# A mixture-of-experts kernel whose expert weights pass through a ring of 12 places: 18 places, six experts loaded ahead in place of four, and x1 kept in DRAM

## What is computed

```python
scores = sigmoid(t @ w_router); sel = scores + router_bias     # t: 256 x 1024, 64 experts
# group-limited: 4 of 8 groups, then the top 8 experts of each token
act = silu(g) * u * combine                                    # g, u = split(t @ w_gate_up[e])
routed = sum over experts of act @ w_down[e]                   # 1024x512 and 256x1024 weights per expert
shared = (silu(sg) * su) @ w_shared_down
x = x1 + gate2 * (routed + shared); y = rmsnorm(x, final_norm_g)
```

| experts | tokens |
|---|---|
| 58, 59 | 32, 11 |
| 60 to 63 | 32, 8, 0, 52 |
| the other 58, sorted | 81 79 67 64 / 64 64 64 64 63 60 60 60 59 56 56 54 51 51 46 43 42 42 39 38 35 35 / 34 32 30 29 29 25 25 23 22 22 20 20 17 16 14 14 14 13 13 11 11 10 7 5 5 4 3 3 3 1 1 0 |

## Time and profile before

### The profile page before, as it was taken

The page is one execution under the profiler, slowest core; times in us unless marked ns, Lnnn a source line. Parts: engine busy times, 40 slices in busy tenths (PEclk is TensorE's granted clock), DMA queues, the critical chain, the costliest instruction groups (busy, mean ns, idle before and its releaser), DMA issues.

```text
span 936.0 us, 12460 instructions
## 1 busy us (share of the span) xinstructions
PE 840.4 (90%) x5100; PEld 566.1 (60%) x5100; DVE 361.5 (39%) x719; ACT 199.5 (21%) x314; POOL 107.8 (12%) x69
## 2 busy tenths in 40 slices
PE   4699999998999999999999989699787998779974
PEld 2488998678999988888455434255242553435422
DVE  1327899279798441156212122012121121112214
ACT  3124443033434120033112111011110111101101
POOL 1000628222342210021000000000000000000000
PEclk9799999999899999979999999899898999989987
DMA  8978887222252439731869999999999999999991
GB/s 319 387 266 317 317 287 256 90 90 90 91 180 92 152 117 346 279 134 46 313 266 417 419 416 418 415 418 419 415 418 416 416 420 414 419 415 415 419 401 59
DMA packets 76419, 280.46 MB, mean 300 GB/s; under 512 B 5080, under 2 KB 7496, under 8 KB 59976
## 3 DMA queue, kind: packets, MB, share of 16 engines
q1 hardware_dynamic: 76008, 278.90, 76.2%
q10 hardware_dynamic: 352, 0.74, 0.2%
HBM read 277.52 MB, written 2.10 MB: 299 GB/s over the span
## 4 chain that ended last, share of the span: by engine, by line
PE 76%; DMA 15%; DVE 4%; SPq 2%; issue 2%; ACT 1%; POOL 0%; DVEq 0%; POOLq 0%
PE bank L1766 14%; DMA chunk<-in_w_expert_down 11%; PE bank L1813 11%; PE bank L1417 9%; PE bank L1665 5%; PE bank L1429 5%; PE bank L1431 5%; PE bank L1437 5%; PE bank L1688 4%; PE bank L1472 3%; PE bank L1452 3%; DMA ring<-in_w_ada 2%; PE bank L1385 2%; DMA chunk<-in_w_expert_gate_up 2%; PE bank L1653 2%
## 5 line engine op out<-in xcount | busy, mean ns | idle before, releaser
L1766 PE MATMUL bank<-chunk,xg 128*32 128x512 f32 (+2 forms) x1024 | 193.6, 627 | 25.9 <-DMA chunk<-in_w_expert_gate_up 25.5
L1766 PEld LDWEIGHTS bank<-chunk,xg 128*32 128x32 f32 (+2 forms) x1024 | 63.8, 131 | 152.7 <-issue 138.4
L1813 PE MATMUL bank<-chunk,act_t 128*32 128x512 f32 (+2 forms) x512 | 108.3, 710 | 26.2 <-DMA chunk<-in_w_expert_down 22.2
L1270 DVE SCALAR_TENSOR_TENSOR act_r<-bank,w_slot,sil 128x256 f32<-128x256 f32 x26 | 12.6, 484 | 190.1 <-ACT sil L837 190.1
L1813 PEld LDWEIGHTS bank<-chunk,act_t 128*32 128x32 f32 (+2 forms) x512 | 33.0, 143 | 81.4 <-issue 81.3
L571 POOL TENSOR_TENSOR small<-small 128x4 f32<-128x4 f32 (+2 forms) x9 | 10.2, 1136 | 607.4 <-DVE small L1326 502.8
L1282 DVE TENSOR_TENSOR y_lo<-bank,y_hi 128x512 fp32r<-128x512 f32 x52 | 36.0, 692 | 107.5 <-ACT y_hi L850 107.5
L850 ACT ACTIVATE y_hi<-bank 128x512 fp32r<-128x512 f32 x52 | 31.1, 597 | 125.0 <-PE bank L1813 125.0
L837 ACT ACTIVATE sil<-bank 128x256 f32<-128x256 f32 x26 | 10.0, 385 | 205.7 <-PE bank L1766 205.7
L1665 PE MATMUL bank<-sel_p,h_hi 128*128 128x256 f32 x208 | 52.7, 294 | 0.9 <-DVE act_s L1226 0.9
L961 DVE SCALAR_TENSOR_TENSOR conv<-upad,dw,conv 128x256 f32<-128x256 f32 x120 | 51.2, 501 | 0.0
(11 more groups left out here) (269 smaller groups left out, 1318.9 us busy)
## 6 DMA issues: line engine op xcount, KB each, us to landing
chunk<-in_w_expert_gate_up SPq DMA_DIRECT2D x128, 1024.0 KB, 17.2
chunk<-in_w_expert_down SPq DMA_DIRECT2D x64, 1024.0 KB, 18.6
ring<-in_w_in SPq DMA_DIRECT2D x16, 2048.0 KB, 10.5
ring<-in_w_ada SPq DMA_DIRECT2D x12, 2048.0 KB, 14.2
ring<-in_w_proj_hgrn SPq DMA_DIRECT2D x2, 2048.0 KB, 8.0
ring<-in_w_out SPq DMA_DIRECT2D x2, 2048.0 KB, 12.8
ring<-in_w_proj_conv SPq DMA_DIRECT2D x1, 2048.0 KB, 7.7
w_sg<-in_w_shared_gate_up SPq DMA_DIRECT2D x1, 2048.0 KB, 9.7
```

Source lines behind the costliest of these rows:

```text
L1766: ins = mm(bank[2 + b][e * width:(e + 1) * width, :], xg[:, k, c:c + width], w[:, k % 4, :], start=(k == 0), stop=(k == KD - 1))
L1813: ins = mm(out[e * width:(e + 1) * width, :], act_t[:, c, e * width:(e + 1) * width], w[:, c, h * 512:(h + 1) * 512], start=(c == 0), stop ...
```

## The change

The ring gets 18 places, at addresses given one by one in `PLACES`. Six experts are fixed, in three steps; 58 are ranked, with 4, 22 and 32 of them in the three widths. `STEPS` keeps its 26 steps and sums (four of width 128, fourteen of 64, eight of 32) in another order. The shared expert's down weights become piece 48, just ahead of those of step 6, and its product moves from step 1 to step 6. `x1` is written to a DRAM tensor and read back after the last piece, as `fin_g` is; `g2row` is formed in steps 24 and 25.

```diff
-FIXED, WIDE, MIDDLE, NARROW = 4, 4, 24, 32
+FIXED, WIDE, MIDDLE, NARROW = 6, 4, 22, 32
-STEPS = [64, 64] + [32, 128, 64, 64, 32, 64] * 4
+FIXED_STEPS = FIXED // 2
+STEPS = [64] * FIXED_STEPS + [32, 64, 32, 128, 64, 32, 64, 64, 32, 128, 64, 32, 64, 64, 32, 128, 64, 32, 64, 128, 32, 64, 64]
...
-NCHUNK = 12
+NCHUNK = 18
+SHARED_STEP = 6
 CHUNK_NO = {}
 for n_step, n_items in enumerate(ITEMS_OF):
+    if n_step == SHARED_STEP:
+        CHUNK_NO["shared"] = len(CHUNK_NO)
     for n_part in range(3):
         for n_item in range(n_items):
             CHUNK_NO[n_step, n_part, n_item] = len(CHUNK_NO)
 CHUNK_AT = {number: key for key, number in CHUNK_NO.items()}
...
+PLACES = [152, 112, 120, 80, 88, 0, 8, 144, 16, 24, 72, 32, 40, 48, 56, 160, 168, 64]
+AFTER_SHARED = (15, 16)
+EXTRA_PLACES = 12
+LOADS_BEFORE_EXTRAS = (len(CHUNK_NO) - EXTRA_PLACES) // NCHUNK + 1
...
-        chunk = [at(f"chunk{i}", 8 * i, [P, 2048]) for i in range(NCHUNK)]
-        h_hi = at("h_hi", 112, [P, NS, KD, P], F32R)
-        h_lo = at("h_lo", 120, [P, NS, KD, P], F32R)
-        x1 = at("x1", 128, [P, NS, D])
-        xg = at("xg", 144, [P, KD, 2 * P])
+        chunk = [at(f"chunk{i}", PLACES[i], [P, 2048]) for i in range(NCHUNK)]
+        x1_out = at("x1_out", 128, [P, NS, D])
+        h_lo = at("h_lo", 128, [P, NS, KD, P], F32R)
+        h_hi = at("h_hi", 136, [P, NS, KD, P], F32R)
+        xg = at("xg", 96, [P, KD, 2 * P])
...
-        w_sg = at("w_sg", 144, [P, KD, 2 * FF])
-        w_sd = at("w_sd", 104, [P, 2, D])
+        w_sg = at("w_sg", 160, [P, KD, 2 * FF])
...
-        fin = at("fin", 96, [P, NS, D])
-        fin_sq = at("fin_sq", 112, [P, NS, D])
+        fin = at("fin", 48, [P, NS, D])
+        fin_sq = at("fin_sq", 56, [P, NS, D])
+        g2row = at("g2row", 64, [P, NS, D])
+        fin_g = at("fin_g", 160, [P, D])
+        x1 = at("x1", 168, [P, NS, D])
...
-            first = 3 * NE // NCHUNK - NIT
-            eng.wait_ge(s_chunk[extra_place(b, part, item)], i * 16 + 16 * (first + 1))
+            eng.wait_ge(s_chunk[extra_place(b, part, item)], i * 16 + 16 * (LOADS_BEFORE_EXTRAS + 1 - NIT))
...
-                               ("t1", 4, "act"), ("g2", 4, "act"), ("hr", 4, "act"), ("sg", 1, "act"), ("su", 1, "dve")]):
+                               ("t1", 4, "act"), ("hr", 4, "act"), ("sg", 1, "act"), ("su", 1, "dve")]):
...
-                if name == "ph1":
-                    evacuated(sp, "st", 3)
-                    sp.dma_start(new_state[0, 0].rearrange("a h k v -> k (a h) v"), s_new[:, :, :]).then_inc(s_state, 16)
...
+            evacuated(sp, "st", 3)
+            sp.dma_start(new_state[0, 0].rearrange("a h k v -> k (a h) v"), s_new[:, :, :]).then_inc(s_state, 16)
+            sp.dma_start(w_sg[:, :, :], cols(A["w_shared_gate_up"][0], 0)).then_inc(s_sg, 16)
...
             for number in range(NCHUNK):
-                step, part, item = CHUNK_AT[number]
-                if number == 0:
+                if number in AFTER_SHARED:
+                    continue
+                if number == 1:
+                    sp.wait_ge(o_ready, 4)
+                if number == 4:
                     sp.wait_ge(ob_used, 4)
-                if number == 2:
+                if number == 5:
                     released(sp, "ph0")
-                if number == 4:
+                if number == 7:
                     released(sp, "ph1")
-                    sp.dma_start(w_sg[:, :, :], cols(A["w_shared_gate_up"][0], 0)).then_inc(s_sg, 16)
-                    sp.dma_start(fin_g[:, :], A["final_norm_g"].rearrange("(a d) -> a d", a=1).broadcast_to([P, D])).then_inc(s_fing, 16)
-                if number == 6:
+                if number == 10:
                     sp.wait_ge(merged, 4)
-                if number == 7:
+                if number == 11:
                     released(sp, "wo0")
-                if number == 9:
+                if number == 13:
                     released(sp, "wo1")
-                load_part(number, part, FIRST_FIXED + sum(ITEMS_OF[:step]) + item)
+                load_fixed(number)
+            evacuated(sp, "t1", 3)
+            sp.dma_start(A["x1"].rearrange("s p d -> p s d"), x1_out[:, :, :]).then_inc(s_x1_kept, 16)
             filled(sp, "su")
-            sp.dma_start(w_sd[:, :, :], A["w_shared_down"][0].rearrange("(k p) c -> p k c", p=P)).then_inc(s_sd, 16)
+            for number in AFTER_SHARED:
+                load_fixed(number)
 
...
+                if CHUNK_AT[number] == "shared":
+                    sp.wait_ge(shared_done, 1)
+                    return
...
-            for step in range(2, NSTEPS):
+            for step in range(FIXED_STEPS, NSTEPS):
+                if step == SHARED_STEP:
+                    number = CHUNK_NO["shared"]
+                    freed(number - NCHUNK)
+                    sp.dma_start(dn_tile(place_of(number)), A["w_shared_down"][0].rearrange("(c p) d -> p c d", p=P)).then_inc(s_chunk[place_of(number)], 16)
...
+            for number in (max(n for n in CHUNK_AT if place_of(n) == at_) for at_ in (15, 16)):
+                freed(number)
+            sp.dma_start(fin_g[:, :], A["final_norm_g"].rearrange("(a d) -> a d", a=1).broadcast_to([P, D])).then_inc(s_fing, 16)
+            sp.wait_ge(s_x1_kept, 16)
+            sp.dma_start(x1[:, :, :], A["x1"].rearrange("s p d -> p s d")).then_inc(s_x1_back, 16)
...
+                if j == 0:
+                    pool.wait_ge(s_x1_kept, 16)
...
-            for name, dst in (("t1", x1), ("g2", g2row)):
-                if name == "g2":
-                    act.wait_ge(spread2, 1)
-                    nc.scalar.activation(inv2[:, :], bank[5][:, 0:T], ACT.Copy).then_inc(inv2_done, 1)
-                for s in range(NS):
-                    for hf in range(2):
-                        filled(act, name, 2 * s + hf)
-                        nc.scalar.activation(dst[:, s, hf * 512:(hf + 1) * 512], fill_bank(name, 2 * s + hf)[:, :], ACT.Copy).then_inc(act_evac, 1)
+            for s in range(NS):
+                for hf in range(2):
+                    filled(act, "t1", 2 * s + hf)
+                    nc.scalar.activation(x1_out[:, s, hf * 512:(hf + 1) * 512], fill_bank("t1", 2 * s + hf)[:, :], ACT.Copy).then_inc(act_evac, 1)
+            act.wait_ge(spread2, 1)
+            nc.scalar.activation(inv2[:, :], bank[5][:, 0:T], ACT.Copy).then_inc(inv2_done, 1)
...
+            def second_gate(j):
+
+                act.wait_ge(g2_ready, j + 1)
+                nc.scalar.activation(g2row[:, j // 2, j % 2 * 512:(j % 2 + 1) * 512], bank[0 if j == 3 else 1][:, :], ACT.Copy).then_inc(g2_evac, 1)
...
             for n in range(NSTEPS):
+                if n == NSTEPS - 2:
+                    second_gate(0)
+                    second_gate(1)
+                if n == NSTEPS - 1:
+                    second_gate(2)
+                    second_gate(3)
...
+            dve.wait_ge(s_x1_back, 16)
+            dve.wait_ge(g2_evac, 4)
...
-            for j in range(4):
-                s, hf = j // 2, j % 2
-                b = open_fill("g2", j)
-                for i in range(4):
-                    ins = mm(b[:, i * P:(i + 1) * P], mod_v[:, M_GT2 + 4 * hf + i, s:s + 1].broadcast_to([P, P]), ident, start=True, stop=True)
-                ins.then_inc(proj_ready, 1)
...
-            def scatter(b, s, h, last=False):
+            def scatter(b, s, h, first=False, last=False):
                 for part in (y_hi, y_lo):
-                    ins = mm(y_acc[s][h][:, :], sel_t[b][:, s * P:(s + 1) * P], part[h][:, :], start=False, stop=(last and part is y_lo))
+                    ins = mm(y_acc[s][h][:, :], sel_t[b][:, s * P:(s + 1) * P], part[h][:, :], start=(first and part is y_hi), stop=(last and part is y_lo))
...
-                pe.wait_ge(items_done, 2)
-                pe.wait_ge(s_sd, 16)
+                number = CHUNK_NO["shared"]
+                pe.wait_ge(s_chunk[place_of(number)], 16 * (number // NCHUNK) + 16)
+                w_sd = dn_tile(place_of(number))
                 for s in range(NS):
                     for hf in range(2):
                         for c in range(2):
-                            mm(y_acc[s][hf][:, :], act_s[:, c, s * P:(s + 1) * P], w_sd[:, c, hf * 512:(hf + 1) * 512], start=(c == 0), stop=False)
+                            ins = mm(y_acc[s][hf][:, :], act_s[:, c, s * P:(s + 1) * P], w_sd[:, c, hf * 512:(hf + 1) * 512], start=False, stop=False)
+                ins.then_inc(shared_done, 1)
+
+            def second_gate(j):
+
+                s, hf = j // 2, j % 2
+                if j == 3:
+                    pe.wait_ge(pt_evac, NSTEPS)
+                elif j:
+                    pe.wait_ge(g2_evac, j)
+                for i in range(4):
+                    ins = mm(bank[0 if j == 3 else 1][:, i * P:(i + 1) * P], mod_v[:, M_GT2 + 4 * hf + i, s:s + 1].broadcast_to([P, P]), ident, start=True, stop=True)
+                ins.then_inc(g2_ready, 1)
 
             def gather_next(i, weights):
...
```

(46 more changed lines are left out.)

39 lines of the change are left out of this document (19 added, 20 removed).

## The result

The changed kernel takes **957.05 us** (median of 4 runs, 955.62 to 958.5) against 937.45 for the kernel before in 4 runs: ratio 1.0204, interval 1.0183 to 1.0226. It is slower by 19.6 us; 957.0 was forecast. The runs of the changed kernel spread over 2.9 us. The profiled execution is the fastest of them: 955.62 us, span 953.5.

A forecast was written before the change was run, and what follows sets the result against it. Expert-weight DMA, not TensorE, was taken to bound half the span. Step 25's down at 903.1 plus 37.6 for the round gives 940.7; 15.0 behind it gives span 955.7, or 957.0 us on the median, range 949 to 970.

The forecast's parts named there:

- idle DMA at 475 to 485: Queue hole early in the experts' stream: moving the shared product makes it 7.1 us less, leaving some 2 us.
- step 25's down ends: End of the 26 regular steps on TensorE: at 903.1, 17.9 us earlier than 920.97.
- entry into the round: After step 25: its results, reading nwork and branching, a gather and turn; 6.2 us, bounds 5 and 8.
- the round's two steps: Extra-item steps on TensorE: 14.1 us for the first and 13.5 without a gather, 27.6 us.
- eight rounds passed over: Unused rounds of the extra-item loop, counted ahead of the last down: 3.8 us, bounds 0 and 9.4.
- the whole round: One round of extra items for two overflowing tokens after step 25: 37.6 us, range 32.6 to 45.
- behind the last down: Results, norm and stores from the last down to the span's end: 15.0 us, as before.
- 5 us of cover for the round's pieces: The round's 12 pieces, 30.2 us of DMA, land at 930.3 before the last down at about 935, so they hide.
- punctual pieces: Low-bound term: pieces land without the 3.4 us lateness allowed at the stream's end, -2.6 us.
- rival 2: Each round passed over stalls TensorE's instruction stream: 970 us, 987 if both jumps stall; middle 975, chance 0.06.
- Rival 1: No extra round runs, as rank 26's expert has at most 32 tokens or the branch is not taken: 919.3, chance 0.07.
- Rival 3: The deeper ring is not full by 448 because SP waits earlier; 12.6 us gain lost: 970 us, chance 0.04.

The follow-up runs named there:

- experiment 7: The kernel before with the second gate's four groups moved to steps 24 and 25: 935.56 us, ratio 0.9997.
- experiment 1: The changed kernel without the round of extra items, leaving out two of one expert's 34 tokens: 916.91 us, ratio 0.9805.
- experiment 2: The kernel before with 1 added to nwork, so one round runs on items that hold no token: 971.85 us, ratio 1.0406.
- experiment 10: The changed kernel timed again, unaltered, against the kernel before: 955.47 us, ratio 1.0213.
- experiment 3: The changed kernel with NX = 4 in place of 36, so the loop has one round and none is passed over: 949.84 us, ratio 1.0163.
- experiment 4: The changed kernel with 4 added to nwork, so two rounds run, the second without tokens: 985.99 us, ratio 1.054.
- experiment 6: The kernel before with the shared expert's down product moved from step 1 to step 6: 930.37 us, ratio 0.9935.
- experiment 5: The changed kernel without the round, two tokens left out, with 12 pieces loaded early in place of 18, ring still 18: 923.03 us, ratio 0.9863.

## Why the prediction was right

| step of the prediction | predicted | measured |
|---|---|---|
| start of the stream | 447.9, as before | 446.25 |
| idle DMA at 475 to 485 | 2 us (7.1 less) | 0.9 us |
| step 25's down ends | 903.1 | 901.16 |
| last byte of the round's pieces | 926.9 | 926.3 |
| the second gate in steps 24 and 25 | 1 + 2 groups of 0.93 us in the sum | 1.09 and 1.98 us in the chain, but no cost in experiment 7 |
| entry into the round | 6.2 us (5 to 8) | 5.2 us |
| the round's two steps | 27.6 us | 27.9 us |
| eight rounds passed over | 3.8 us (0 to 9.4) | 3.98 us; in place of 0.48, so 3.5 us more |
| the whole round | 37.6 us | 37 to 38 us by experiments 1, 2 and 10 |
| without it | 919.3 (17.9 us under before) | 17.9 us under before by the medians, 18.3 (15.4 to 21.2) by the ratio |
| last down ends | 940.7 | 934.30 |
| behind the last down | 15.0 us | 19.2 us |
| span | 955.7 | 953.5 in the profiled run, the fastest of four |

The mechanism was the one forecast. The decisive step was not in the trace's timing but in its counts: 1024 records said that nothing overflowed before, and the sorted counts said that one expert, with 34 tokens in a width of 32, overflows now. Experiment 1 shows that this alone turns a gain of 17.9 us into a loss of 19.6. The sums agree to a microsecond partly by luck: the start of the stream and step 25 came out 1.7 and 1.9 us early, and the profiled span is 2.2 us below the predicted one, while the median run is 1.4 us above the profiled one.

Two things lie elsewhere than the prediction has them. It counts the rounds passed over ahead of the last down, and as a sign of being right it asks for some 38 us from step 25's down to the last one; there are 33.1, and the rounds passed over come behind. That, the 1.9 us of step 25, 1.0 us of the entry and -0.3 of the two steps are the 6.4 us by which the last down came early. And it has no term for the last scatter at half clock, 0.9 us, behind those rounds. Of its 5 us of cover for the round's pieces, the last down had 4.3 (its first product starts at 930.63, the last byte comes at 925 + 5 x 111/417 = 926.3), but the second half of gate and up in the same step had none and waited 0.19 us.

Two of its numbers lack their working: punctual pieces are put at -2.6 us, where their lateness is 3.4, and rival 2's 987 is sixteen transfers of 2.1 us less the 3.8 already counted, not twice 13.

Rival 1 fell by the 1088 records. Rival 2 fell by experiments 3 and 4: a round passed over costs 0.5 to 0.56 us, on VectorE, and no instruction stall of PE adds to it, for in the five profiled runs with rounds passed over PE's first product starts 0.11 or 0.12 us after the memset that releases it. The prediction's estimate from the Trainium skill (Advanced Engine Details and Errata, section Control Flow Timing), about 2 us for eight rounds, is half of the 3.98 us measured; the measurement decides. Rival 3 fell by SP's queue: its last two pieces left at 435.92 at the latest.

Where the gain without the round comes from can be read from the windows of experiment 1:

```profile
890.00:895.00 5.00, 5.00 (x24) 2.16 (x21) 0.48 (x1) 0.39 (x1) 0.00 (x0) 1.00 0.86 345
895.00:900.00 5.00, 4.43 (x22) 1.81 (x20) 0.69 (x1) 0.98 (x2) 0.00 (x0) 1.00 0.13 51
```

Its last byte comes at 890 + 5 x (345 + 51)/417 = 894.7, less 3.8 us for `fin_g` and x1, so 890.9 for the experts, 21.7 us ahead of 912.6. Five pieces less are 12.6 us of this, less idle queue 6.3, and the earlier start of the stream (445.17 for 447.93) 2.8, which the prediction put at nothing and which is no more than two runs of one kernel differ by. The experiments bound these parts only roughly: the hole is 3.7 to 8.3 us by experiment 6, the six pieces early some 2 to 9 by experiment 5. How much the ring of 18 gives with twelve pieces early in the old kernel, and how much the new order of the steps gives, was not run.

## What to carry to other kernels

A capacity fixed at build time is part of a kernel's cost: before changing how many experts are fixed or how wide the ranks are, compare the sorted counts with the widths one by one, for here two tokens cost 37 us, twice what the rest of the change gains. The count of records in the trace tells at once whether the overflow path ran. Where a loop of rounds is made for the worst case, the rounds passed over are paid as well, some 0.5 us each, and once more by the engine that stands idle meanwhile. Where early loads are the gain, look at when the order is known and when the first place comes free: a deeper ring can fill idle queue between the two, as in experiment 5.

## What was not expected of the hardware

**SP is held up by its own issues when places are not short.** Before, the median issue of a piece took 0.33 to 0.38 us, and from 520 to 870 us SP waited 195.9 us for TensorE to free places; in the change it waited 3.2 us there, and the issue itself takes 1.08 and 2.16 us, and up to 6.9. The view of the tile `chunk`, min, median and max in ns:

```profile
L559 SPq DMA_DIRECT2D chunk<-in_w_expert_gate_up x124: 332/1077/4317, 446.3 to 904.0; - x124
L559 SPq DMA_DIRECT2D chunk<-in_w_expert_down x62: 373/2156/6880, 464.0 to 906.2; - x62
...
DMA to landing us min/median/max: 4.9/21.7/28.1
```

21.7 us from issue to landing at 2.514 us a piece are some 9 pieces under way, against 17.7 us and 7 before. That more places beyond these would only wait at SP was not tried.

**Runs of one kernel start the stream at different times, and most of the difference is made in the first 50 us.** The changed kernel was profiled twice, in the result and in experiment 10. Its router starts at 408.78 and at 405.45, and its stream at 446.25 and at 442.13. The windows of the first weights and the router's first product, in the result and then in experiment 10:

```profile
10.00:50.00 40.00, 32.62 (x154) 19.60 (x155) 11.03 (x34) 10.65 (x18) 0.70 (x1) 0.70 1.05 388
408.78 7.52 PE L1687 MATMUL bank<-w_r,h_t 128*128 128x64 f32 x32 [4.93 <-DVE h_t L1171]
```

```profile
10.00:50.00 40.00, 32.76 (x173) 21.38 (x173) 11.04 (x34) 11.79 (x21) 0.70 (x1) 0.96 1.05 388
405.45 7.51 PE L1687 MATMUL bank<-w_r,h_t 128*128 128x64 f32 x32 [4.93 <-DVE h_t L1171]
```

The granted clock there is 0.70 and 0.96: PE has many idle gaps in this stage and goes between the full clock and half of it. The first products of `h_t` with the next weights start at 41.9 and 38.8, already 3.1 us apart. The first output projection starts at 340.5 and 337.2, 3.3 us apart, and the router follows it by 68.3 us in both; another 0.8 us come between the router and the stream, with a mean clock of 0.50 and 0.72 from 408 to 420 us. Over the nine profiled runs of kernels with the changed first part, the clock from 10 to 50 us was 0.59 to 0.96 and the router started at 411.89 to 405.45, in nearly the same order. That the clock is the cause was not tested. It means that times of single profiled runs from different kernels, as those of experiments 1 and 5, compare only to some 4 us before the start of the stream is taken out.
